# Storing x early, and adding the last scaled tiles to the output by transfers of GpSimd's queue

## The chip, the cores and the metric

The kernel runs on one core of a Trainium2 chip. Its time is the device time of one execution in microseconds (us); lower is better. The kernel before took 1996.66 us, the median of three runs (1994.56 to 1998.79). A profile shows one further execution.

## The reference, cut to what matters

Two layers work on x, 512 tokens by 1024 features in float32. Each layer has three sub-layers, a token mixer, a cross-attention into 256 memory tokens and a squared-ReLU feed-forward, and each of them ends in the same way:

```
def rms_norm(x, g):
    y = xf * lax.rsqrt(jnp.mean(xf * xf, axis=-1, keepdims=True) + NORM_EPS)
    return y * g
...
        h = rms_norm(x, ffn_pre_g[i])
        x = x + rms_norm(squared_relu_mlp(h, w_up[i], w_down[i]), ffn_post_g[i])
    return x
```

So the output is x as it stood before the last feed-forward, plus the feed-forward's result y, scaled for each token by one over its root mean square and for each feature by a gain. The change touches only this last sum.

## The kernel before, in words

Everything is kept with features on the 128 partitions: `x_sb` and `y_sb` are eight tiles (KT = 8) of 128 features by 512 tokens, each tile 256 KB. The output in memory has the same layout (128 partitions, 8 tiles, 512 tokens), so one tile is 2 KB of contiguous bytes in a partition and two neighbouring tiles are 4 KB. There are six post-norms, numbered 0 to 5, three for each layer; post-norm 5 is that of the last feed-forward.

The program is written out by hand, engine by engine, with semaphores:

- SyncE (SP) issues nearly all transfers. Its queue in order: the inputs, then the weights unit by unit (`load_unit`, L344; 512 KB a transfer into four buffers `raw`, each refilled when VectorE has read it), the memory tokens (L367), and at the very end eight stores of x (L403), each after a wait for `x_ready`, which VectorE's addition of that tile raises. Then it waits until all eight have landed (`out_done`).
- TensorE multiplies in units of 96 matmuls (L1330). Behind the last unit it sums the squares of y over features with a matrix of ones (`statistic`, L1354).
- ScalarE splits weights (L504), squares the tiles of y (L816), and makes `rstd` of the summed squares in `root`, a logarithm (L547) and an exponential (L550).
- VectorE forms the low parts of the weights (L838), adds the partial products of the feed-forward into `y_sb` (L1257), and at the end calls `post_normed(5, ...)` eight times. Each call scales one tile of `y_sb` in place (L915, raises `y_scaled`), waits for its own write, and adds it to the tile of `x_sb` (L925, raises `x_ready`). In all earlier post-norms the same function is used, and what follows reads `x_sb`.
- GpSimd adds squares (L419) and the rotated halves of queries and keys (L434). It issues no transfer anywhere in the kernel before; its last work is three additions of squares in the last feed-forward.

The order of the work around the change is: last unit of TensorE, its last partial products added to y by VectorE, squares by ScalarE, `statistic`, `root`, eight pairs of scaling and addition, and the stores that follow them tile by tile.

`wait_added(engine, post, k)` is a wait for `x_ready` to reach 8 * post + k + 1. After post-norm 4, the cross-attention's of the second layer, nothing changes `x_sb` until post-norm 5.

Of the kernel before, what the change touches and what calls it, by code (L numbers as in the profile page):

```python
# [25 lines left out]
KT = D // P  # L26
# [112 lines left out]
def build(nc, x, mem, positions, gains, consts, lam, subln_g, da_w_qkv, da_w_o, db_w_qkv, db_w_o,  # L139
# [3 lines left out]
    ALU = mybir.AluOpType  # L143
# [6 lines left out]
    with ExitStack() as ctx:  # L150
# [3 lines left out]
        def sem(name):  # L154
            return ctx.enter_context(nc.semaphore(name))


        x_sb = sb("x_sb", [P, KT, S])
        y_sb = sb("y_sb", [P, KT, S])
# [11 lines left out]
        rstd = sb("rstd", [P, S])  # L171
# [62 lines left out]
        y_scaled = sem("y_scaled")  # L234
# [21 lines left out]
        tables = sem("tables")  # L256
        lam_sums = sem("lam_sums")
        lam_exp = sem("lam_exp")
        out_done = sem("out_done")

        class Attention:

# [65 lines left out]
        def wait_added(engine, post, k):  # L328

            engine.wait_ge(x_ready, KT * post + k + 1)  # L330
# [4 lines left out]
        @block.sync  # L335
        def _(sp):
            def load_unit(u, w, row_pair, col, ii=0, pairs=range(4)):

                for j in pairs:
                    if u > 0:  # L340

                        sp.wait_ge(w_lo_ready, ii * 8 + (4 * u + j - 3))
                    src = w[bass.ds(row_pair + j, 1), bass.ds(col, 1)]
                    sp.dma_start(raw[:, j], src[0, 0]).then_inc(raw_loaded[j], 16)  # L344

            sp.dma_start(gain[:, :, :], gains).then_inc(gain_loaded, 16)
            for n, (k, end) in enumerate(X_LOADS):
                sp.dma_start(x_sb[:, k:end, :], x[:, k:end]).then_inc(x_loaded[n], 16)
                w = tiles(da_w_qkv)
                if n in FIRST_PAIRS:  # L350
                    load_unit(0, w, 0, 0, pairs=FIRST_PAIRS[n])
            sp.dma_start(cst[:, :], consts).then_inc(small_loaded, 16)
            sp.dma_start(half[:, 0, :].bitcast(i32), positions.broadcast_to([P, S])).then_inc(small_loaded, 16)
            sp.dma_start(half[:, 1, 0:4 * DA_DQ],
                         lam.broadcast_to([P, 4 * DA_DQ])).then_inc(small_loaded, 16)
            sp.dma_start(subg[:, 0:1], subln_g).then_inc(small_loaded, 16)
            for n in range(1, 6):
                load_unit(n, w, 0, n)

            def after_attention(layer, att):  # L360

                u = UNITS[f"o{layer}"]
                w = tiles(da_w_o if layer == 0 else db_w_o)
                load_unit(u, w, 0, 0)

                sp.wait_ge(att.weighed, att.n)
                sp.dma_start(mem_sb[:, :, :], mem).then_inc(mem_loaded, 16)  # L367
                load_unit(u + 1, w, 0, 1)
                w = tiles(xa_wkv[layer])
                for n, col in enumerate((2, 3, 0, 1)):  # L370
                    load_unit(UNITS[f"kv{layer}"] + n, w, 0, col)
                for name, w in (("xq", xa_wq), ("xo", xa_wo)):
                    for n in range(2):
                        load_unit(UNITS[f"{name}{layer}"] + n, tiles(w[layer]), 0, n)
                u = UNITS[f"ff{layer}"]
                up, down = tiles(w_up[layer]), tiles(w_down[layer])
                load_unit(u, up, 0, 0)
                with sp.Fori(0, CHUNKS - 1) as c:
                    load_unit(u + 1, up, 0, c * 2 + 1, c * 2)
                    for n in range(2):  # L380
                        load_unit(u + 2 + n, down, c * 4, n, c * 2)
                    load_unit(u + 4, up, 0, c * 2 + 2, c * 2)
                u += 4 * (CHUNKS - 1)
                load_unit(u + 1, up, 0, 2 * CHUNKS - 1)
                for n in range(2):
                    load_unit(u + 2 + n, down, 4 * (CHUNKS - 1), n)

            after_attention(0, att_d)
            w = tiles(db_w_qkv)
            for h in range(2):  # L390
                u = UNITS["qkv1a" if h == 0 else "qkv1b"]
                load_unit(u, w, 0, h)
                with sp.Fori(0, GROUPS - 1) as g:
                    load_unit(u + 1, w, 0, g * 2 + (2 * GROUPS + h), g)
                    load_unit(u + 2, w, 0, g * 2 + (2 + h), g)
                load_unit(u + 2 * GROUPS - 1, w, 0, 4 * GROUPS - 2 + h)
                for g in range(GROUPS):
                    load_unit(u + 2 * GROUPS + g, w, 0, 4 * GROUPS + 2 * g + h)
            after_attention(1, att_l[1])
            for k in range(KT):  # L400

                wait_added(sp, 5, k)
                sp.dma_start(out[:, k], x_sb[:, k, :]).then_inc(out_done, 16)  # L403
            sp.wait_ge(out_done, 16 * KT)


        @block.gpsimd
        def _(pool):
# [31 lines left out]
            for layer in range(2):  # L440
                for k in range(KT):
                    square_sum(f"mem{layer}", k, mem_sq)
                for k in range(POOLED[f"mix{layer}"]):
                    square_sum(f"mix{layer}", k, sq)
                for k in range(POOLED[f"xa{layer}"]):
                    square_sum(f"xa{layer}", k, sq)

                wait_added(pool, 3 * layer + 1, KT - 1)
                pool.wait_ge(rstd_ready, STATS[f"fpre{layer}"] + 1)
                nc.gpsimd.memset(y_sb[:, :, :], 0.0).then_inc(y_cleared, 1)  # L450
                if layer == 0:
                    nc.gpsimd.memset(mask[:, :, 0:S + P], 0.0).then_inc(mask_step, 1)
                    steps = 1
                    for r in range(DIL):

                        for at, width, step, base in ((0, S, DIL, r), (S, P, 1, 0)):
                            part = mask[:, r, at:at + width]
                            for sign in (1, -1):
                                pool.wait_ge(mask_step, steps)
                                nc.gpsimd.affine_select(out=part, in_=part, compare_op=ALU.is_ge, fill=MASKED,  # L460
                                                        base=RADIUS - sign * base, pattern=[[sign, width]],
                                                        channel_multiplier=-sign * step).then_inc(mask_step, 1)
                                steps += 1

                        if r == 0:
                            pool.wait_ge(phase_ready, 1)
                        for a in range(2):
                            far = mask[:, r, S + P + a * 64:S + P + (a + 1) * 64].rearrange("p (a b) -> p a b", b=DIL)
                            nc.gpsimd.tensor_copy(far, phase4[:, :].rearrange("p (o b) -> p o b", o=1)
                                                  .broadcast_to([P, 16, DIL])).then_inc(mask_step, 1)  # L470
                            steps += 1
                    assert steps == MASK_STEPS

                for k in range(POOLED[f"ff{layer}"]):
                    square_sum(f"ff{layer}", k, sq)
                if layer == 0:
                    for name in ("qkv1a", "qkv1b"):
                        u = UNITS[name]

                        def rope_sums(kind, g, ii):  # L480
                            for m in range(HALF):
                                rope_sum(banks_out(u + kind, m, ii), (u + kind) % 2,
                                         (k1 if kind % 2 else q1)[:, g, m, :], m)

                        rope_sums(0, slice(0, 1), 0)
                        with pool.Fori(0, GROUPS - 1) as g:
                            rope_sums(1, bass.ds(g, 1), g)
                            rope_sums(2, bass.ds(g + 1, 1), g)
                        rope_sums(2 * GROUPS - 1, slice(GROUPS - 1, GROUPS), 0)


        @block.scalar
# [332 lines left out]
        def _(dve):  # L825
# [82 lines left out]
            scalings_of_y = 0  # L908
# [233 lines left out]
            for layer in range(2):  # L1142
                if layer == 1:
                    for h in range(2):
# [16 lines left out]
                        if h == 0:  # L1161
                            dve.wait_ge(mask_step, MASK_STEPS)
                        for g in range(GROUPS):
# [116 lines left out]
                if layer == 0:  # L1280
                    boundary(2, 0, "ffn_post_g", "pre1", 1, "mix_pre_g", UNITS["qkv1a"])
                else:
                    for i in range(KT):
                        post_normed(5, 1, "ffn_post_g", i)

# [312 lines left out]
                statistic(f"ff{layer}")  # L1600


MASK_STEPS = 1 + DIL * 6


# [32 lines left out]
```

## Time and profile before

| | before |
|---|---|
| median of three runs | 1996.66 us |
| the profiled execution's own time | 1997.33 us |
| its span, from the first to the last instruction | 1995.5 us |
| TensorE busy | 1930.1 us, 97% of the span |
| VectorE busy | 1000.9 us, 50% |
| ScalarE busy | 738.5 us, 37% |
| GpSimd busy | 187.1 us, 9% |
| bytes moved | 167.32 MB |

The span is what the profile's clock covers; the execution's own time is 1.83 us longer, and it lies 0.67 us above the median of the runs. A point of time in the rows below is counted from the start of the span.

### The profile page before, as it was taken

Reading aid. Unit: us, or ns where it says so; the run is one execution under the profiler, and the core shown is the slowest. Engines: PE = TensorE matmul, PEld = TensorE weight load, DVE = VectorE, ACT = ScalarE, POOL = GpSimd, SP = SyncE. Lnnn points to the kernel's source line nnn. Section 1 sums busy time; section 2 is a strip of 40 time slices with the busy share of each in tenths; the row PEclk is TensorE's granted clock in tenths of the full one; section 3 lists DMA queues with packets and bytes.
Section 4 is the critical chain, followed back from the end, with each engine's and each line's share of the span. In section 5 each row is a group of like instructions: output and inputs, shape, how many; then the busy total and the mean of one; then the engine's idle time right before and its main releaser. Section 6 shows DMA issues by size and latency. Waiting matters only on the chain.

```text
span 1995.5 us, 23552 instructions
## 1 busy us (share of the span) xinstructions
PE 1930.1 (97%) x8970; PEld 1582.9 (79%) x8970; DVE 1000.9 (50%) x1369; ACT 738.5 (37%) x1148; POOL 187.1 (9%) x139
## 2 busy tenths in 40 slices
PE   8999999999999999989999999999999999999996
PEld 6785578887888888768899888898788868888885
DVE  5958937444534334476623365333474354334444
ACT  4127846334413223332124321244453343223232
POOL 0410021000300000013300033100300000000000
PEclk9999999999999999999999999999999999999998
DMA  4320034302232223323321133310352122322331
GB/s 157 95 86 10 1 106 154 110 24 76 91 95 95 95 95 96 94 74 95 95 85 43 29 94 101 95 42 5 129 173 74 43 76 93 95 95 95 95 95 53
DMA packets 85654, 167.32 MB, mean 84 GB/s; under 512 B 5568, under 2 KB 5696, under 8 KB 85312
## 3 DMA queue, kind: packets, MB, share of 16 engines
q1 hardware_dynamic: 85568, 166.15, 26.9%
q8 instruction: 57, 0.93, 0.2%
q14 instruction: 29, 0.24, 0.0%
HBM read 164.03 MB, written 2.10 MB: 83 GB/s over the span
## 4 chain that ended last, share of the span: by engine, by line
PE 86%; DVE 6%; ACT 4%; issue 2%; POOL 1%; DMA 0%; SPq 0%; ACTq 0%; DVEq 0%; POOLq 0%
PE ps L1330 74%; PE ps L1354 2%; PE ps L1499 2%; PE ps L1390 1%; DVE half L880 1%; DVE w_lo L838 1%; PE ps L1489 1%; PE ps L1492 1%; PE ps L1553 1%; PE ps L1434 1%; DVE small L1036 1%; PE ps L1545 1%; PE ps L1428 1%; ACT w_hi L504 1%; PE ps L1314 1%
## 5 line engine op out<-in xcount | busy, mean ns | idle before, releaser
L838 DVE TENSOR_TENSOR w_lo<-raw,w_hi 128x1024 fp32r<-128x1024 f32 x304 | 377.9, 1244 | 740.6 <-ACT w_hi L504 738.7
L504 ACT ACTIVATE w_hi<-raw 128x1024 fp32r<-128x1024 f32 x304 | 321.7, 1058 | 906.2 <-PE ps L1330 900.5
L1330 PE MATMUL ps<-act_hi,w_lo 128*128 128x512 f32 x1392 | 547.4, 393 | 5.7 <-DVE w_lo L838 4.0
L1330 PE MATMUL ps<-act_lo,w_hi 128*128 128x512 f32 x1408 | 548.2, 391 | 0.0
L1330 PE MATMUL ps<-act_hi,w_hi 128*128 128x512 f32 x1392 | 541.9, 389 | 0.0
L1330 PEld LDWEIGHTS ps<-act_hi,w_lo 128*128 128x128 f32 x1392 | 261.6, 188 | 64.4 <-DVE w_lo L838 5.7
L1330 PEld LDWEIGHTS ps<-act_lo,w_hi 128*128 128x128 f32 x1408 | 266.2, 189 | 57.0 <-issue 1.9
L1330 PEld LDWEIGHTS ps<-act_hi,w_hi 128*128 128x128 f32 x1392 | 261.3, 188 | 54.7
L1330 PE MATMUL ps<-ff_hi,w_lo 128*128 128x512 f32 x512 | 201.7, 394 | 0.0
L1330 PE MATMUL ps<-ff_lo,w_hi 128*128 128x512 f32 x512 | 201.7, 394 | 0.0
L1330 PE MATMUL ps<-ff_hi,w_hi 128*128 128x512 f32 x512 | 201.7, 394 | 0.0
L419 POOL TENSOR_TENSOR sq<-sq 128x512 f32<-128x512 f32 x26 | 39.0, 1500 | 956.9 <-ACT sq L816 616.1
L1330 PEld LDWEIGHTS ps<-ff_lo,w_hi 128*128 128x128 f32 x512 | 95.7, 187 | 23.7
L1330 PEld LDWEIGHTS ps<-ff_hi,w_lo 128*128 128x128 f32 x512 | 95.8, 187 | 23.7
L1330 PEld LDWEIGHTS ps<-ff_hi,w_hi 128*128 128x128 f32 x512 | 95.7, 187 | 23.6
L880 DVE TENSOR_TENSOR half<-ps,sin_sb 64x512 f32<-64x512 f32 (+1 forms) x160 | 110.1, 688 | 2.2
L1330 PE MATMUL ps<-w_hi,act_lo 128*128 128x512 f32 x256 | 102.7, 401 | 0.0
L1330 PE MATMUL ps<-w_hi,act_hi 128*128 128x512 f32 x256 | 102.0, 399 | 0.0
L1330 PE MATMUL ps<-w_lo,act_hi 128*128 128x512 f32 x256 | 102.0, 398 | 0.0
L434 POOL TENSOR_TENSOR q<-q,half 128x512 f32<-128x512 f32 (+1 forms) x32 | 58.4, 1824 | 319.6 <-DVE half L880 319.6
L1330 PEld LDWEIGHTS ps<-w_hi,act_lo 128*128 128x128 f32 x256 | 64.4, 251 | 6.1 <-issue 0.8
L1330 PEld LDWEIGHTS ps<-w_hi,act_hi 128*128 128x128 f32 x256 | 64.5, 252 | 5.3
(155 smaller groups left out, 2134.4 us busy)
## 6 DMA issues: line engine op xcount, KB each, us to landing
raw<-in_db_w_qkv SPq DMA_DIRECT2D x72, 512.0 KB, 3.8
raw<-in_w_up SPq DMA_DIRECT2D x64, 512.0 KB, 3.8
raw<-in_w_down SPq DMA_DIRECT2D x64, 512.0 KB, 3.8
raw<-in_xa_wkv SPq DMA_DIRECT2D x32, 512.0 KB, 3.9
raw<-in_da_w_qkv SPq DMA_DIRECT2D x24, 512.0 KB, 3.7
raw<-in_xa_wq SPq DMA_DIRECT2D x16, 512.0 KB, 3.9
raw<-in_xa_wo SPq DMA_DIRECT2D x16, 512.0 KB, 3.7
raw<-in_da_w_o SPq DMA_DIRECT2D x8, 512.0 KB, 3.7
```

Of the source, the lines that this page charges most:

```text
L419: nc.gpsimd.tensor_tensor(squares[:, 0, :], squares[:, 0, :], squares[:, k, :], ALU.add).then_inc(sq_summed, 1)
L434: nc.gpsimd.tensor_tensor(dst, dst, half[:, n % 2:n % 2 + 1, :], ALU.add).then_inc(rope_done, 1)
L504: nc.scalar.activation(w_hi[:, g % 2], raw[:, g % 4], ACT.Copy).then_inc(w_hi_ready, 1)
L838: nc.vector.tensor_tensor(w_lo[:, g % 2], raw[:, g % 4], w_hi[:, g % 2].bitcast(f32), ALU.subtract).then_inc(w_lo_ready, 1)
L880: last = nc.vector.tensor_tensor(half[to:to + swap, m % 2:m % 2 + 1, :], src[at:at + swap], sin_sb[at:at + swap], ALU.mult)
L1036: nc.vector.tensor_reduce(small[:, t % 2, 2:2 + count], scores, AX.X, ALU.max, negate=True).then_inc(a.taken, 1)
L1314: nc.tensor.matmul(ps[:, s + m, :], weights[:, 0, 0, c], hi[:, 0], start=(weights is w_hi), stop=False)
L1330: last = nc.tensor.matmul(ps[:, s + m, 0:width], left, right, start=(k == 0 and n == 0 and not early), stop=(k == KT - 1 and n == 2))
L1354: last = nc.tensor.matmul(ps[:, stat_bank(name), 0:width], ones[:, :], squares[:, k, :], start=(k == order[0]), stop=(k == order[-1]))
L1390: last = nc.tensor.transpose(a.turn_banks(n, b), a.e[:, n % (a.lag + 1), b * P:(b + 1) * P], ident[:, :])
L1428: last = nc.tensor.matmul(ps[:, 2 * (t % 2) + c, :], q0[r, h, s * P:(s + 1) * P], k0[r, h, :], start=True, stop=True)
L1499: last = nc.tensor.matmul(ps[:, a.out_bank(h), r * P:(r + 1) * P], v1[:, g, tile, h * P:(h + 1) * P], p_of(a, n, b), start=(b == 0), stop= ...
```

## The change

SyncE no longer stores eight tiles behind eight additions. As soon as its weight loads are issued it waits for the last tile of post-norm 4 and stores the whole of `x_sb`, 2 MB, in one transfer (`x_stored`). VectorE's last loop only scales: eight instructions on `y_sb`, without a wait between them and without the additions into `x_sb`. GpSimd, behind its last additions of squares, waits until x has landed, and then for each pair of scaled tiles issues a transfer of 512 KB that adds `y_sb` to what stands in the output. Four of these are counted in `out_added`, for which SyncE waits at the end. The number of scalings that `y_scaled` has counted before the last loop is written down as a constant, 32.

```diff
-            for k in range(KT):
-
-                wait_added(sp, 5, k)
-                sp.dma_start(out[:, k], x_sb[:, k, :]).then_inc(out_done, 16)
-            sp.wait_ge(out_done, 16 * KT)
+            wait_added(sp, 4, KT - 1)
+            sp.dma_start(out, x_sb[:, :, :]).then_inc(x_stored, 16)
+            sp.wait_ge(x_stored, 16)
+            sp.wait_ge(out_added, 16 * (KT // 2))
...
+            pool.wait_ge(x_stored, 16)
+            for k in range(0, KT, 2):
+                pool.wait_ge(y_scaled, SCALED_BEFORE_LAST + k + 2)
+                nc.gpsimd.dma_start(out[:, k:k + 2], y_sb[:, k:k + 2, :], accum_op=ALU.add).then_inc(out_added, 16)
...
                 else:
+                    assert scalings_of_y == SCALED_BEFORE_LAST
                     for i in range(KT):
-                        post_normed(5, 1, "ffn_post_g", i)
+                        nc.vector.scalar_tensor_tensor(
+                            y_sb[:, i, :], y_sb[:, i, :], gcol(1, "ffn_post_g", i), rstd[:, :],
+                            ALU.mult, ALU.mult).then_inc(y_scaled, 1)
...
+SCALED_BEFORE_LAST = 4 * KT
```

## Rows read from the trace of the kernel before

**Rows 1.** The page's first part: busy time, share of the span and instructions.

```profile
PE 1930.1 (97%) x8970; PEld 1582.9 (79%) x8970; DVE 1000.9 (50%) x1369; ACT 738.5 (37%) x1148; POOL 187.1 (9%) x139
```

**Rows 2.** The chain that ended last, from 1980 us: start us, us, what.

```profile
1980.50 0.70 ACT rstd L547
...
1981.22 0.64 ACT rstd L550
...
1981.89 0.76 DVE y_sb L915
...
1982.67 0.69 DVE x_sb L925
1983.37 0.67 DVE y_sb L915
...
1992.40 0.69 DVE x_sb L925
```

**Rows 3.** SyncE's waits from 1980 us: queue, line, releaser, total, times, longest.

```profile
SPq L403 <- DVE x_sb L925: 45.2, 8, 38.0
SPq L150 <- DMA out<-x_sb: 1.7, 1, 1.7
```

**Rows 4.** The output's transfers: duration ns, first and last start us; then time to landing.

```profile
L403 SPq DMA_DIRECT2D out<-x_sb x8: 332/332/361, 1983.4 to 1993.1; - x8
...
DMA to landing us min/median/max: 2.0/2.0/2.0
```

**Rows 5.** Short windows of the last store: us, busy engines, PEclk, DMA share, GB/s.

```profile
1993.60:1993.80 0.20, 0.00 (x0) 0.00 (x0) 0.00 (x0) 0.00 (x0) 0.00 (x0) 0.50 0.00 0
1993.80:1994.00 0.20, 0.00 (x0) 0.00 (x0) 0.00 (x0) 0.00 (x0) 0.00 (x0) 0.50 0.21 82
1994.00:1994.20 0.20, 0.00 (x0) 0.00 (x0) 0.00 (x0) 0.00 (x0) 0.00 (x0) 0.50 1.07 410
...
1994.40:1994.60 0.20, 0.00 (x0) 0.00 (x0) 0.00 (x0) 0.00 (x0) 0.00 (x0) 0.50 0.97 369
1994.60:1994.80 0.20, 0.00 (x0) 0.00 (x0) 0.00 (x0) 0.00 (x0) 0.00 (x0) 0.50 0.23 72
```

**Rows 6.** Windows of the start, where many transfers queue; columns as in rows 5.

```profile
5.00:10.00 5.00, 1.58 (x4) 1.32 (x5) 1.89 (x2) 2.56 (x4) 0.00 (x0) 1.00 1.02 390
10.00:15.00 5.00, 5.00 (x16) 3.94 (x15) 3.41 (x5) 5.00 (x9) 0.00 (x0) 1.00 1.03 383
```

**Rows 7.** SyncE's queue from 1900 us, in time: start us, us, what, count.

```profile
1906.56 38.83 SPq L344 DMA_DIRECT2D raw<-in_w_down  x8
1983.39 10.05 SPq L403 DMA_DIRECT2D out<-x_sb  x8
```

**Rows 8.** Transfers by line: count, KB each, median us from issue to landing.

```profile
raw<-in_w_down SPq DMA_DIRECT2D x64, 512.0 KB, 3.8
...
mem_sb<-in_mem SPq DMA_DIRECT2D x2, 1024.0 KB, 4.9
out<-x_sb SPq DMA_DIRECT2D x8, 256.0 KB, 2.0
x_sb<-in_x SPq DMA_DIRECT2D x3, 512.0 KB, 7.4
```

**Rows 9.** ScalarE in time from 1950 us: start us, us, line, what, idle before.

```profile
1965.07 1.06 ACT L504 ACTIVATE w_hi<-raw 128x1024 fp32r<-128x1024 f32 x1 [3.50 <-PE ps L1330]
```

**Rows 10.** GpSimd in time, from 46 us and from 1646 us; columns as in rows 9.

```profile
46.08 1.30 POOL L434 TENSOR_TENSOR q<-q,half 128x512 f32<-128x512 f32 x1 [44.42 <-DVE half L880]
49.60 2.34 POOL L434 TENSOR_TENSOR q<-q,half 128x512 f32<-128x512 f32 x1 [2.22 <-DVE half L880]
...
1966.73 3.24 POOL L419 TENSOR_TENSOR sq<-sq 128x512 f32<-128x512 f32 x2 [3.79 <-ACT sq L816]
```

**Rows 11.** VectorE in time beside those of rows 10; columns as in rows 9.

```profile
46.73 2.79 DVE L880 TENSOR_TENSOR half<-ps,sin_sb 32x512 f32<-32x512 f32 x4
49.55 1.23 DVE L838 TENSOR_TENSOR w_lo<-raw,w_hi 128x1024 fp32r<-128x1024 f32 x1
```

More of the change, by code:

```diff
@@ L258, in build @@
         lam_exp = sem("lam_exp")
-        out_done = sem("out_done")
+        x_stored = sem("x_stored")
+        out_added = sem("out_added")
         class Attention:
```

## The prediction

> **What bounds the kernel now.** I read the page's first part first: the matmul engine is busy for 97% of the span [rows 1], so nothing shortens the kernel but less matmul work or a shorter stretch without matmuls, and the change leaves all matmuls alone. The second view is the chain that ended last, at its end. The reader is to see there that behind the last statistic ScalarE's two steps of the root stand, then one scaling and one addition of VectorE in turn, with nothing between them, from 1981.89 us until the last addition ends at 1992.40 + 0.69 = 1993.09 [rows 2]. The third view is SyncE's waits: each of the eight stores waited for its addition, and at the end SyncE waited 1.7 us for the last store to land [rows 3]. So the tail is VectorE's chain, 11.20 us, then one store of 256 KB: issued at 1993.1 and landed 2.0 us later, at 1995.1 [rows 4]; 0.4 us of closing follow to the span's 1995.5. The question is only how 13.2 us, from 1981.89 to 1995.1, come out in another form.
>
> Windows of the last store split its 2.0 us [rows 5]: no byte until about 1993.95, some 0.85 us behind the issue; then about 0.7 us of movement near 400 GB/s; then 0.45 us to the landing. At the start of the kernel, where transfers queue, reads hold 383 to 390 GB/s over 10 us [rows 6]. I take 394 GB/s as the most that this core's transfers move, since shares of 0.97 to 1.07 in both views say that the transfer engines are full there.
>
> **The change, part by part.**
>
> *VectorE.* Eight additions of 0.69 us and the short gaps ahead of them go. Eight scalings stay. The first takes 0.75 to 0.76 us, and a following one adds 0.67 to the chain [rows 2], so tiles are ready at 1982.64 + 0.67 n: the first pair at 1983.31, then 1984.65, 1985.99 and the last at 1982.64 + 7 x 0.67 = 1987.33. That is 1993.09 - 1987.33 = 5.76 us earlier than the last addition before. If the overlap is lost, at 0.76 each, the last is ready at 1987.97.
>
> *The early store of x.* SyncE's last weight load is issued at 1906.56 + 38.83 = 1945.4 [rows 7]; the store of 2 MB follows at once, since post-norm 4 is long past. At 394 GB/s it moves for 5.3 us; with a load ahead of it (3.8 us to landing [rows 8]) and the fixed parts of rows 5 it lands by about 1956. GpSimd waits for it, behind its additions that end at 1966.73 + 3.24 = 1969.97 [rows 10], and it first needs x in the output at 1983.31, so there are 27 us to spare. What else could it disturb? Only the last weight tiles: the last of them is read at 1965.07 [rows 9], nearly 20 us after its load was issued. I cost the store at nothing; its cover is the last unit's matmuls, and without it the cost would be the 5.3 us and the fixed parts. The eight stores that it replaces were under VectorE's chain but the last, which is the 2.0 us above. Nothing is queued behind GpSimd's new waits but these transfers, and nobody waits for them but SyncE at the end.
>
> *The four adding transfers.* No row shows a transfer of GpSimd's queue, or one that adds. I need two prices.
>
> First, from issue to first byte. The nearest row is SyncE's store, 0.85 us [rows 5]; that is the low end of what I take. GpSimd has to prepare the transfer itself. The high end is 0.85 plus 1.4, by the longest that one of its plain additions of 128x512 takes alone (1.30 us [rows 10]). I take 0.85 + 0.9 = 1.75. Only the first counts if the transfers then queue: preparation goes on under the one before.
>
> Second, the movement t of 512 KB. Low end: a plain copy, 524288 / 394000 = 1.33 us. An adding transfer reads y from the core's memory and also the old output, two reads for one write. If the reading side of the 16 engines carries both, t is 2 x 1.33 = 2.66 us. High end: the slowest 512 KB of the trace, x's loads at 7.4 us to landing in a full queue [rows 8], less 1.3 us of fixed parts, so 6.1. I take 2.66, because the rows show transfer engines that are full at 394 GB/s of plain copies, and a second read can't be free for a full engine; it is nearer to the low end.
>
> The Trainium skill bears on this. Its page Collectives: The Full Stack (The bandwidth ceiling: the fold count and why AG ≠ RS ≠ AR) says that a reduction in the transfer engines is half as fast as a copy because it reads two sources through the same queue, and not because the addition costs. The trace has no adding transfer to agree or disagree; by that rule the sum is the one below, without it t would be open between its ends.
>
> *The sum.* First byte at 1983.31 + 1.75 = 1985.06. Transfers of 2.66 us are slower than the 1.34 us in which VectorE delivers a pair, so they queue: end at 1985.06 + 4 x 2.66 = 1995.70. Add 0.45 to land and 0.4 of closing: 1996.55, against 1995.5. VectorE's 5.76 us are given back, because 2 MB of additions now begin only when the first pair is scaled. The change in the span is +1.05 us; with the short end of the start (0.85) it is +0.15, with the long one +1.55. The profiled execution took 1997.33 us, 1.83 over its span, so it becomes 1998.4; it stood 0.67 above the median, so against the runs I say 1997.7, rounded to 1998.
>
> A measurement of this kernel can tell about 0.2%, 4 us, from no change: "same" reaches from 1992.7 to 2000.7. The change is even where t is (1995.5 - 0.85 - 1985.06) / 4 = 2.40 us, and slower by 4 us from t = 3.40.
>
> **The rivals.**
>
> *A, the transfers keep up (faster).* Reads of the two sources run side by side and t is 1.33. Then each pair's transfer is done when the next pair is ready, and only the last counts: 1987.33 + 1.75 + 1.33 + 0.45 + 0.4 = 1991.26, 4.2 us less, 1992.4 against the median; with a start as short as SyncE's, 1991.5. For it: stores one after another already reach 390 GB/s, and reading and writing are two sides of an engine. Against it: full shares in rows 5 and 6.
>
> *B, the adding is slow (slower).* Each 4 KB row is read, added and written at half the rate again, t = 5.3 us, by waiting for the old value before the write or by a slow adder. End: 1985.06 + 21.3 + 0.85 = 2007.2, 11.7 us more, 2008.4. It decides from t = 3.4 us. For it: x's 512 KB loads took 7.4 us in a full queue, and no row shows that reads and writes of the same bytes overlap. Against it: plain transfers, in rows 5 and 6, run at full share in either direction.
>
> *C, VectorE locks GpSimd out (slower).* The trace shows such a lock: an addition of GpSimd took 1.30 us beside a VectorE instruction with one input from PSUM, and 2.34 us where it began with L838, which has both inputs in SBUF; it took 1.04 us more, about what was left of L838 when it began [rows 10, 11]. The eight scalings have two such inputs and stand without a gap. If they hold up GpSimd's preparation, the first byte comes at 1987.33 + 1.75 = 1989.08 and the end at 1989.08 + 10.64 + 0.85 = 2000.6, 5.1 us more, 2001.7. Against it: GpSimd was held in a reading instruction there. The Trainium skill (SBUF — State Buffer, Who interferes with whom) says that a VectorE instruction with two inputs in SBUF holds up GpSimd's reads, not instructions that only write; rows 10 agree with its first half (2.34 us for 1.30), and no row shows the second. By it C doesn't happen.
>
> *D, the change doesn't do what it says.* The early store isn't landed at 1983.31 and everything slides. It would have to take over 37 us; 2 MB at 394 GB/s take 5.3.
>
> **How the numbers follow.** The forecast (t near 2.7) 0.45, A 0.15, B 0.28, C 0.09, D 0.03. B has much, since the price of adding is the one number that no row bounds well, and nothing hides it. Predicted time 1998. A gives 1992.4, so the range begins at 1992; B gives 2008.4 and a little above it, so it ends at 2010; A with the shortest start and B with t over 5.7 are left out. The forecast's own range, t from 2.4 to 3.4, is 1997 to 2001. Faster by over 0.2% is A, 0.15; within it is the forecast, 0.45; slower is B, C and D, 0.40.
>
> **What the changed profile would show.** VectorE's last scaling ends near 1987.3 and no addition into x_sb follows it. The store of 2 MB starts near 1945.4 and lands before 1960. GpSimd's first transfer is issued within 0.1 us of 1983.3, and under C at 1987.3 or with nothing moving before it. The share of the transfer engines is full from about 1985.1 to 1995.7; under A there are gaps between four short bursts of 1.3 us, under B a stretch of over 20 us. TensorE's stretch to 1980.5 is unchanged. I am wrong if the four transfers take less than 2.4 us each, or more than 3.4, or if they leave gaps though pairs are ready, since then it is GpSimd's preparation that sets the pace.

## The result: slower by 0.17%, with the transfers at half rate as forecast and a lag that was not

Twenty runs of each kernel: 2001.71 us median after (1997.28 to 2003.82), 1997.55 us before (1994.41 to 1999.70). The ratio is 1.0017 with a 95% interval from 1.0011 to 1.0024, so 3.4 us slower, between 2.2 and 4.8; the two medians lie 4.2 us apart. The profiled execution took 2002.83 us with a span of 2001.0.

The two profiled executions differ by 1.6 us before the tail even starts: the root ends at 1983.43 us in one and at 1981.86 in the other. Over all fourteen profiles of this study that point lies between 1978.8 and 1983.4 us, and even the two of the changed kernel differ by 1.8. So I compare tails, from the end of the root to the end of the span. The changed kernel's is 2001.0 - 1983.43 = 17.6 us, that of before 1995.5 - 1981.86 = 13.6 us: 3.9 us longer (differences of tails are taken before rounding), which the timed ratio bears out.

The changed kernel's chain of waits, its end (start us, us, what), which answers to [rows 2]:

```profile
1982.79 0.64 ACT rstd L555
...
1983.45 0.75 DVE y_sb L1290
1984.20 0.66 DVEq L150
1984.87 2.66 DVE y_sb L1290 x4
1987.53 0.28 issue
1987.81 0.84 POOL out L494
1988.65 0.46 issue
1989.12 0.88 POOLq L150
```

The reader is to see that the additions (L925 before) are gone, and that the chain passes to GpSimd and then stops at 1990.0, 11 us ahead of the end: the rest is movement of bytes, which no engine's chain shows. GpSimd's and VectorE's instructions in time, and then the output's transfers with their time to landing, against [rows 4]:

```profile
1983.45 5.39 DVE L1290 SCALAR_TENSOR_TENSOR y_sb<-y_sb,gain,rstd 128x512 f32<-128x512 f32 x8 [4.98 <-ACT rstd L555]
...
1985.50 1.90 POOL L494 DMA_DIRECT2D out<-y_sb  x2 [13.97 <-DVE y_sb L1290]
1987.81 0.84 POOL L494 DMA_DIRECT2D out<-y_sb  x1 [0.41 <-DVE y_sb L1290]
1989.14 0.86 POOL L494 DMA_DIRECT2D out<-y_sb  x1 [0.48 <-DVE y_sb L1290]
```

```profile
L494 POOL DMA_DIRECT2D out<-y_sb x4: 840/878/1000, 1985.5 to 1989.1; - x4
L402 SPq DMA_DIRECT2D out<-x_sb x1: 467/467/467, 1947.0 to 1947.0; - x1
...
DMA to landing us min/median/max: 5.8/9.1/11.4
```

Eight scalings take 5.39 us (5.44 forecast). The last adding transfer is issued at 1989.1 and lands 11.4 us later. Windows of the tail, whose last two columns are the transfer engines' share and the GB/s, against [rows 5]. A window counts a packet whole where it starts, so a share can pass 1, and does so most in the short window in which the first packets of all engines start together:

```profile
1986.80:1987.00 0.20, 0.00 (x0) 0.00 (x0) 0.20 (x2) 0.00 (x0) 0.20 (x1) 0.50 0.00 0
1987.00:1987.20 0.20, 0.00 (x0) 0.00 (x0) 0.20 (x1) 0.00 (x0) 0.20 (x1) 0.50 4.10 307
...
1987.00:1989.00 2.00, 0.00 (x0) 0.00 (x0) 1.84 (x3) 0.00 (x0) 1.24 (x2) 0.50 1.07 129
1989.00:1998.00 9.00, 0.00 (x0) 0.00 (x0) 0.00 (x0) 0.00 (x0) 0.86 (x1) 0.50 1.04 200
1998.00:2000.00 2.00, 0.00 (x0) 0.00 (x0) 0.00 (x0) 0.00 (x0) 0.00 (x0) 0.50 0.11 20
```

The last three of these lines are the result. From 1989 to 1998 us the share is full (1.04) while only 200 GB/s move, half of the 394 at which the same engines copy. Ahead of that stand 2 us at 129 GB/s, and behind it 2 us in which a share of 0.11 moves the last 40 KB. One engine of the 16 is a share of 0.06.

The trace also keeps every packet of the transfers, here one for each 4 KB row. A plain packet takes 0.162 us in the median (plain copies from the same queue, below), an adding one 0.328: the factor of two again. But 39 of the 512 adding packets take over 0.43 us, all of them in the first 6 us of movement, and the longest takes 2.41 us. The last six packets follow one after another, from 1998.36 to 2000.24 us. The trace doesn't say which engine a packet belongs to; that the last ones are the backlog of an engine which such a long packet held up is my reading of it.

### The profile page after: what moved, and what is told of

Its sections match the earlier page's. It is cut to its first block, busy times and chain, and to the rows that moved or that the text cites. A ratio compares the mean times of both kernels' runs of the same rounds, so it can differ in the third digit from the quotient of the medians.

```text
span 2001.0 us, 23543 instructions
## 1 busy us (share of the span) xinstructions
PE 1931.3 (97%) x8970; PEld 1583.9 (79%) x8970; DVE 995.4 (50%) x1361; ACT 738.5 (37%) x1148; POOL 190.7 (10%) x143
## 4 chain that ended last, share of the span: by engine, by line
PE 86%; DVE 6%; ACT 4%; issue 2%; POOL 1%; DMA 0%; POOLq 0%; DVEq 0%; SPq 0%; ACTq 0%
PE ps L1338 74%; PE ps L1362 2%; PE ps L1507 2%; PE ps L1398 1%; DVE half L885 1%; DVE w_lo L843 1%; PE ps L1497 1%; PE ps L1500 1%; PE ps L1561 1%; PE ps L1442 1%; DVE small L1041 1%; PE ps L1553 1%; PE ps L1436 1%; PE ps L1322 1%; ACT w_hi L509 1%
```

## The experiments

My theory was the forecast's: an adding transfer fills the engines and gets half a copy's rate, so 2.1 MB need over 10 us, and that stands on the path since it can't begin before the first pair is scaled. The rivals: GpSimd's queue is slow for any transfer; VectorE's scalings hold up GpSimd's preparation; the early store costs time; each transfer has a price of its own. A table of all comes first. The tail is from one profile each; the last column is what the timed ratio makes of 1997.6 us. The two kernels of plain copies leave the addition of x out. Where nothing else is said a ratio rests on eleven runs of the kernel named (twenty of the changed one), against runs of the kernel before taken beside them: on seven for plain copies from SyncE, five for adding when all is scaled, four for plain loads beside. Where tails are compared with each other, 0.6 us is what two profiles of one kernel differ by.

| kernel | ratio (95% interval) | tail us | tail less 13.6 | by ratio, us |
|---|---|---|---|---|
| changed | 1.0017 (1.0011 to 1.0024) | 17.6; again 18.2 | +3.9; +4.6 | +3.4 |
| plain copies, GpSimd's queue | 0.9981 (0.9972 to 0.9990) | 10.0 | -3.7 | -3.8 |
| plain copies, SyncE's queue | 0.9973 (0.9962 to 0.9985) | 8.4 | -5.2 | -5.4 |
| adding only when all is scaled | 1.0036 (1.0022 to 1.0050) | 21.0 | +7.3 | +7.2 |
| before, with the early store | 0.9998 (0.9989 to 1.0007) | 13.6 | 0.0 | -0.4 |
| two transfers of four tiles | 1.0017 (1.0008 to 1.0026) | 17.0 | +3.4 | +3.4 |
| eight transfers of one tile | 1.0012 (1.0003 to 1.0022) | 16.5 | +2.8 | +2.4 |
| two tiles by adding transfer | 0.9990 (0.9981 to 0.9999) | 12.2 | -1.4 | -2.0 |
| four tiles by adding transfer | 1.0005 (0.9996 to 1.0014) | 14.8 | +1.2 | +1.0 |
| plain loads beside | 1.0044 (1.0029 to 1.0059) | 21.0 | +7.4 | +8.8 |
| TensorE adds eight tiles | 1.0012 (1.0003 to 1.0021) | 15.4 | +1.8 | +2.4 |
| TensorE adds five tiles | 0.9992 (0.9983 to 1.0001) | 11.6 | -2.0 | -1.6 |

**Plain copies from GpSimd's queue.**

```diff
-                nc.gpsimd.dma_start(out[:, k:k + 2], y_sb[:, k:k + 2, :], accum_op=ALU.add).then_inc(out_added, 16)
+                nc.gpsimd.dma_start(out[:, k:k + 2], y_sb[:, k:k + 2, :]).then_inc(out_added, 16)
```

> The changed kernel with its four transfers made plain copies: y overwrites the output, the addition of x is left out. Tail is meant from the end of the root (rstd) to the end of the span: 13.6 us before, 17.6 us after. Theory (an adding transfer reads two sources, so full transfer engines give half the rate): the four copies move at 380 to 400 GB/s, 1.3 us each, keep up with VectorE's pairs, and the tail is 10 to 12 us, some 6 us under the changed kernel. Rival (the software queue is slow for any transfer): still near 205 GB/s, tail 16 to 18 us.

Its windows (columns as above):

```profile
1987.00:1990.50 3.50, 0.00 (x0) 0.00 (x0) 0.32 (x1) 0.00 (x0) 0.53 (x1) 0.50 0.96 380
1990.50:1990.80 0.30, 0.00 (x0) 0.00 (x0) 0.00 (x0) 0.00 (x0) 0.00 (x0) 0.50 0.91 369
1990.80:1991.00 0.20, 0.00 (x0) 0.00 (x0) 0.00 (x0) 0.00 (x0) 0.00 (x0) 0.50 0.08 21
```

The same bytes from the same queue in the same pieces move at 380 GB/s, and the end is sharp: no lag. The tail is 10.0 us. No packet takes over 0.24 us. So it is the adding that halves the rate and that brings the long packets and the lag, and not GpSimd's queue. The theory stands, that rival falls.

**Plain copies from SyncE's queue.**

```diff
+            for k in range(0, KT, 2):
+                sp.wait_ge(y_scaled, SCALED_BEFORE_LAST + k + 2)
+                sp.dma_start(out[:, k:k + 2], y_sb[:, k:k + 2, :]).then_inc(out_added, 16)
...
-            pool.wait_ge(x_stored, 16)
-            for k in range(0, KT, 2):
-                pool.wait_ge(y_scaled, SCALED_BEFORE_LAST + k + 2)
-                nc.gpsimd.dma_start(out[:, k:k + 2], y_sb[:, k:k + 2, :], accum_op=ALU.add).then_inc(out_added, 16)
```

> As the plain copies of y from GpSimd's queue, but issued by SyncE in the same pairs behind the same scalings; the addition of x is left out. It separates GpSimd's queue from the shape. Theory: same movement, 1.3 us each; the first byte comes 0.85 us behind the issue and nothing lags at the end, so the tail is about 5.4 + 0.85 + 1.33 + 0.45 + 0.4 = 8.4 us. If GpSimd's queue costs nothing more than SyncE's, both kernels of plain copies have the same tail.

```profile
1986.00:1990.00 4.00, 0.00 (x0) 0.00 (x0) 2.47 (x4) 0.00 (x0) 0.00 (x0) 0.50 1.00 400
```

The tail is 8.4 us, as expected. The two kernels of plain copies differ by 1.6 us: that is the price of GpSimd's queue on this path. Most of it is the time from issue to landing of a transfer, 2.7 us in the median here and 3.7 there.

**Adding only when all eight tiles are scaled.**

```diff
-                pool.wait_ge(y_scaled, SCALED_BEFORE_LAST + k + 2)
+                pool.wait_ge(y_scaled, SCALED_BEFORE_LAST + KT)
```

> The changed kernel, its four adding transfers issued only when all eight tiles are scaled. Theory (GpSimd's preparation isn't held up by VectorE's scalings): the issues are 0.85 to 0.9 us each as in the changed kernel, and the whole is later by the 4.0 us that the first issue is later, tail 21.5 us. Rival (VectorE's instructions with two inputs in SBUF hold up the preparation, so that starting early gains little): issues well under 0.85 us, the first byte under 1.6 us behind the first issue, tail 18 to 19 us.

GpSimd in time, in this kernel:

```profile
1987.07 3.65 POOL L494 DMA_DIRECT2D out<-y_sb  x4 [17.95 <-DVE y_sb L1290]
```

and windows of it:

```profile
1988.00:1990.00 2.00, 0.00 (x0) 0.00 (x0) 0.00 (x0) 0.00 (x0) 2.00 (x4) 0.50 0.80 84
1990.00:1999.50 9.50, 0.00 (x0) 0.00 (x0) 0.00 (x0) 0.00 (x0) 0.73 (x1) 0.50 1.05 197
```

With VectorE idle, GpSimd's four preparations take 3.65 us together, 0.9 each (their single records overlap), as they do beside the scalings in the changed kernel, and the first byte comes 1.6 us behind the first issue in both. VectorE doesn't hold them up; the rival called C in the prediction falls. The rate in the middle is much the same, 197 GB/s. The tail is 21.0 us, 3.4 more than the changed kernel's where 4.0 was expected; the end is less ragged here, 1.4 us of lag where the changed kernel has 2.1.

**The early store alone.**

```diff
+            wait_added(sp, 4, KT - 1)
+            sp.dma_start(out, x_sb[:, :, :]).then_inc(x_stored, 16)
+            sp.wait_ge(x_stored, 16)
             for k in range(KT):
...
+                    dve.wait_ge(x_stored, 16)
                     for i in range(KT):
                         post_normed(5, 1, "ffn_post_g", i)
```

> The kernel before with the early store of x alone, and its eight last stores as they were (they overwrite it). Theory: the 2 MB store under the last unit costs nothing, ratio 1.000 within 0.0007, tail 13.6 us. Rival (part of the 4 us is the early store, that delays the last weight tiles or slows the matmuls): 1 to 2 us slower, with a gap in the matmuls after 1946 us.

VectorE's last loop waits here until the early store has landed. Ratio 0.9998, the same tail of 13.6 us. In the changed kernel the store is issued at 1947.0 us and moves from about 1948 to 1955, beside the last weight load and under unbroken matmuls:

```profile
1948.00:1955.00 7.00, 7.00 (x32) 5.61 (x31) 2.61 (x3) 1.06 (x1) 0.00 (x0) 1.00 0.94 367
```

**Four tiles, and one tile, to a transfer.** Only the step of the loop and its counts change (`range(0, KT, 4)`; `range(0, KT, 1)`).

> The changed kernel with two adding transfers of four tiles (1 MB) instead of four of two. Tail from the end of the root to the end of the span, 17.6 us in the changed kernel. Theory (2.1 MB move at some 205 GB/s whatever the cut, and only the first issue's time counts): the first group is ready 1.35 us later, so the tail is 18.9 us. Rival (each of GpSimd's transfers costs time of its own at the start or the end): fewer of them win back 0.9 us or more, tail 18 us or less.

> The changed kernel with eight adding transfers of one tile (256 KB). Theory: the first tile is ready 0.67 us earlier and preparation (0.85 us each in the changed kernel) stays ahead of 1.3 us of movement each, so the tail is 16.9 us. Rival (a price for each transfer, or preparation that sets the pace): 18 us or more, with the transfer engines' share under 0.9 in the middle.

Four tiles: 17.0 us, not the 18.9 of the theory but where the rival was to show (18 or less); the ratio is that of the changed kernel. One tile: 16.5 us, by the theory (16.9 expected) and against the rival (18 or more). A window of four tiles, then those of one tile:

```profile
1988.60:1996.00 7.40, 0.00 (x0) 0.00 (x0) 0.00 (x0) 0.00 (x0) 0.00 (x0) 0.50 1.04 213
```

```profile
1981.00:1983.00 2.00, 0.00 (x0) 0.00 (x0) 2.00 (x4) 0.00 (x0) 2.00 (x5) 0.50 0.66 86
...
1985.00:1993.00 8.00, 0.00 (x0) 0.00 (x0) 0.00 (x0) 0.00 (x0) 2.42 (x3) 0.50 1.11 195
1993.00:1994.00 1.00, 0.00 (x0) 0.00 (x0) 0.00 (x0) 0.00 (x0) 0.00 (x0) 0.50 0.72 129
```

The middle stays near half rate whatever the cut (195, 193 to 200 and 213 GB/s for one, two and four tiles to a transfer). What the cut changes is the two ends, and not in one direction (tails of 16.5, 17.6 to 18.2, 17.0 us). Much of that is the lag. Counted from when fewer than eight packets are under way until the last has ended, it is 0.4 us with one tile, 2.1 and 2.6 in the two profiles with two, and 0.6 with four. A price for each transfer would put eight of them last; they came first. So that rival falls as the explanation of the 3.4 us. The timed intervals of the three kernels overlap, and no order of the cuts is shown.

**Two and four tiles by adding transfer, the others as before.** GpSimd's loop runs to `m`; the early store covers only `out[:, 0:m]`; VectorE scales tiles 0 to m - 1 and then runs `post_normed` for the others, which SyncE stores one by one.

```diff
-            for k in range(0, KT, 2):
+            for k in range(0, 2, 2):
                 pool.wait_ge(y_scaled, SCALED_BEFORE_LAST + k + 2)
...
+                    for i in range(2, KT):
+                        post_normed(5, 1, "ffn_post_g", i)
```

> Mixed: tiles 0 and 1 are only scaled and added by one transfer of GpSimd's queue; tiles 2 to 7 are scaled and added by VectorE and stored by SyncE as in the kernel before. Theory: the adding transfer (2.6 us) is done long before VectorE's last addition, so VectorE's chain sets the end again and is shorter by two additions: 13.6 - 2 x 0.71 = 12.2 us of tail, 1.4 us faster than before, ratio 0.9993. Rival (an adding transfer lags at the end by some us on one engine and delays the stores behind it): 13 us or more.

> Mixed: tiles 0 to 3 by two adding transfers, tiles 4 to 7 by VectorE and SyncE. VectorE's chain would end 2.8 us earlier, at a tail of 10.8 us. Theory (transfer engines at half rate for adding): from the first byte, 3.7 us behind the root, they have 5.3 us of adding and 2.7 us of stores to move, 11.7, and 0.85 to land and close: tail 12.5 us, bound by the transfer engines again, ratio 0.9994. If plain stores overtake the adding transfers, VectorE's 10.8 us show instead.

Two tiles: tail 12.2 us, ratio 0.9990, the only kernel with an addition in transfers that beats the one before, by an interval that ends just under 1 (0.9999) and a tail as expected (12.2). Of its transfers none takes longer than 6.3 us to land, so the adding one, issued at 1982.9, has landed by 1989.2, ahead of the last store's issue at 1990.7. The stores beside it are held up, 3.8 us to landing in the median for 2.0 before, but the last one isn't:

```profile
L407 SPq DMA_DIRECT2D out<-x_sb x6: 332/332/357, 1983.8 to 1990.7; - x6
...
L499 POOL DMA_DIRECT2D out<-y_sb x1: 992/992/992, 1982.9 to 1982.9; - x1
DMA to landing us min/median/max: 2.0/4.5/6.3
```

Four tiles: 14.8 us, not 12.5. Plain stores were expected to queue behind the adding transfers or to pass them. They share the engines, and then the lag is there again; the last packets to move, one at a time, are those of plain stores, which don't get past the adding ones on the engine that is behind:

```profile
1983.00:1985.00 2.00, 0.00 (x0) 0.00 (x0) 1.93 (x4) 0.00 (x0) 1.03 (x2) 0.50 0.72 76
1985.00:1989.00 4.00, 0.00 (x0) 0.00 (x0) 3.31 (x5) 0.00 (x0) 0.00 (x0) 0.50 1.05 203
1990.00:1992.00 2.00, 0.00 (x0) 0.00 (x0) 0.00 (x0) 0.00 (x0) 0.00 (x0) 0.50 1.02 371
1992.00:1994.00 2.00, 0.00 (x0) 0.00 (x0) 0.00 (x0) 0.00 (x0) 0.00 (x0) 0.50 0.18 70
```

The middle of my sum holds (half rate, then plain rate); the two ends, the slow first 2 us (76 GB/s, with some 0.6 us still empty) and the share of 0.18 for the last 2, are what I had not put in.

**Plain loads beside the adding transfers.**

```diff
+            sp.wait_ge(y_scaled, SCALED_BEFORE_LAST + 2)
+            for j in range(4):
+                sp.dma_start(raw[:, j], tiles(w_down[1])[j, 0]).then_inc(beside[j], 16)
+            for j in range(4):
+                sp.wait_ge(beside[j], 16)
```

> The changed kernel, and SyncE issues four plain loads of 512 KB (weights into the free raw buffers) as soon as the first pair is scaled; nothing reads them. Theory (the adding transfers fill the engines, by their two reads): 2.1 MB at 394 GB/s is 5.3 us more to move, and the tail goes from 17.6 to about 22.5 us. Rival (an adding transfer leaves the reading side of an engine idle while it adds, so that plain loads slip in between): tail 18 to 19.5 us, with over 300 GB/s moved in the middle.

21.0 us, between the two: 2.8 to 3.5 us longer than the changed kernel's two tails, where the theory had 5.3 us for the loads. By the timed ratios it is 5.4 us longer (1.0044 for 1.0017, four runs). Its windows:

```profile
1985.00:1990.00 5.00, 0.00 (x0) 0.00 (x0) 2.77 (x5) 0.00 (x0) 3.02 (x4) 0.50 0.95 281
1990.00:2001.00 11.00, 0.00 (x0) 0.00 (x0) 0.00 (x0) 0.00 (x0) 0.00 (x0) 0.50 1.06 233
```

The loads move first, from 1984.9 us, and the first adding packet comes only at 1989.3, 4.9 us behind its issue where the changed kernel has 1.6. After that the engines stay at a full share and move 233 GB/s of both kinds together: a plain transfer finds no room beside an adding one in which it is free. In return the ragged ends are gone. No adding packet takes over 0.72 us, and the lag is 0.3 us; so this tail is shorter than 22.5. This doesn't tell the second read from a slow adder, since either would fill the engine.

**The changed kernel once more.**

> The changed kernel once more, for a second profile of the same code. If the 2 us at the end of its transfers, in which a share of only 0.04 to 0.08 of the transfer engines moved the rest, belong to the kernel, they stand here too and the tail is 17.6 us; if they vary from run to run, the tail is 15.5 to 17 us, by the same 205 GB/s.

```profile
1985.00:1987.00 2.00, 0.00 (x0) 0.00 (x0) 2.00 (x4) 0.00 (x0) 1.41 (x2) 0.50 0.96 113
1987.00:1996.40 9.40, 0.00 (x0) 0.00 (x0) 0.02 (x1) 0.00 (x0) 0.86 (x1) 0.50 1.04 193
1996.40:1999.00 2.60, 0.00 (x0) 0.00 (x0) 0.00 (x0) 0.00 (x0) 0.00 (x0) 0.50 0.11 22
```

The slow start and the lag stand here too (tail 1999.8 - 1981.6 = 18.2 us; 51 packets over 0.43 us, the longest 3.12). They belong to the kernel.

**TensorE adds.** For all eight tiles:

```diff
+            for i in range(KT):
+                if i == KT - 1:
+                    pe.wait_ge(ln_done, STATS["ff1"] + 1)
+                nc.tensor.matmul(ps[:, SUM_BANKS[i], :], ident[:, :], x_sb[:, i, :], start=True, stop=False)
+            for i in range(KT):
+                pe.wait_ge(y_scaled, 4 * KT + i + 1)
+                nc.tensor.matmul(ps[:, SUM_BANKS[i], :], ident[:, :], y_sb[:, i, :],
+                                 start=False, stop=True).then_inc(pe_added, 1)
...
+                    for i in range(KT):
+                        act.wait_ge(pe_added, i + 1)
+                        nc.scalar.activation(x_sb[:, i, :], ps[:, SUM_BANKS[i], :], ACT.Copy).then_inc(x_out, 1)
```

> The kernel before with another way round VectorE's additions: VectorE only scales the eight tiles; TensorE, idle in the tail, adds in PSUM (identity times x ahead of time, then identity times the scaled y), ScalarE copies each sum out and SyncE stores it plainly tile by tile. No early store, no transfer that adds. Theory (what bounded the kernel before was VectorE's chain, and what bounds the changed one is the adding transfers): the last tile is scaled 5.4 us behind the root, plus a matmul of 0.4 to 0.9 us, a copy of 0.65 us, a store of 2.0 us and 0.4 us of closing: tail 9 to 9.5 us, 4 us less than before, ratio 0.998. Rival (TensorE at its lower clock or ScalarE becomes the chain): 10 to 12 us.

A miss: tail 15.4 us. TensorE in time:

```profile
1977.91 7.03 PE L1614 MATMUL ps<-x_sb,ident 128*128 128x512 f32 x16
...
1984.78 7.03 PE L1617 MATMUL ps<-y_sb,ident 128*128 128x512 f32 x16
```

A plain float32 matmul of 128x512 shows as two records and takes 7.03 / 8 = 0.88 us even at the full granted clock (1.00 in these 14 us), so sixteen of them, 14 us, are longer than VectorE's eight additions. I had taken one record, 0.43 us, for the whole, in spite of my upper end of 0.9. TensorE never stood idle here; in the kernel before it did, and the granted clock was 0.50 at the end of the tail [rows 5].

With five tiles on TensorE and three on VectorE (`BY_PE = 5`; SyncE stores in the order 0, 5, 1, 2, 6, 3, 7, 4):

> Where all eight additions ran on TensorE the chain was TensorE's: 16 matmuls in float32 of 0.86 us each. Here TensorE adds five tiles (five matmuls of x from the end of the statistic, then five of the scaled y), VectorE scales these first and then scales and adds the other three, SyncE stores each plainly in the order in which they come. Counted from the end of the root: VectorE's last addition at 0.75 + 4 x 0.67 + 3 x 1.39 = 7.6 us; TensorE's last sum at 10 x 0.86 less the 1.4 us by which it starts earlier, 7.2, and its copy at 7.8. Plus 2.0 us of store and 0.4 of closing: tail 10.2 us against 13.6 before and 17.6 in the changed kernel, so 3.4 us faster than before, ratio 0.9983. If the two chains get in each other's way (stores that queue, TensorE at its lower clock): 11 to 13 us.

The tail is 11.6 us and the ratio 0.9992, whose interval just includes 1: not shown to be faster. The last copy ended 7.8 us behind the root, as worked out. What made it longer than the 10.2 expected was the next thing in line, the stores (their issues and landings, and a window of them):

```profile
L407 SPq DMA_DIRECT2D out<-x_sb x8: 332/461/648, 1983.4 to 1987.2; - x8
...
DMA to landing us min/median/max: 2.1/2.7/3.0
```

```profile
1985.00:1989.00 4.00, 1.15 (x3) 0.19 (x1) 1.52 (x3) 1.26 (x3) 0.00 (x0) 1.00 1.03 383
```

They were ready so close together that they queued: 2.1 MB at 383 GB/s are 5.5 us from the first byte on, and a store landed 2.7 us behind its issue in the median for 2.0 before. From here a shorter tail needs output that leaves earlier, and not only additions that are faster.

## Why the prediction was right, and where it was short

- **What bounds the kernel.** VectorE's chain bounded the tail: plain copies from SyncE with the additions left out save 5.2 us, and the forecast had VectorE 5.76 us earlier.
- **VectorE's part.** The pair was ready 1.44 us behind the root (1.45 forecast), the last tile 5.4.
- **The early store at nothing.** Shown: 0.9998.
- **Half rate.** The step on which everything hung. The forecast took 197 GB/s (2.66 us for 512 KB); 193 to 203 were measured in the full stretches of five profiles (changed kernel twice, all scaled, one tile, four tiles added), against 380 to 400 of plain copies; two transfers of four tiles had 213. By the packet it is 0.328 us for 0.162. The Trainium skill's rule of two source reads (Collectives: The Full Stack, The bandwidth ceiling: the fold count and why AG ≠ RS ≠ AR), which the page states for reductions between cores and not for this path, gives this factor of two. That the cause is the second read and not the adder wasn't shown; the two weren't told apart.
- **Start of the transfers, mis-sized.** From the pair being ready to the first byte: 1.75 us forecast, 2.2 measured (1984.87 to 1987.07). Of it 0.6 us stood ahead of the issue, which the forecast had within 0.1 us of the pair. Then 2 us at 129 GB/s in place of 197 cost another 0.7.
- **End of the transfers, the term that was missing.** I closed the sum with 0.45 + 0.4 us, the plain store's, and let all engines end together. The closing held: 0.8 us from the end of the last packet. Ahead of it stood 2.2 us of lag, for which the sum had no term. The sum by measured terms: 3.6 to the first byte, 11.0 to 1998.0, 2.2 of lag, 0.8 at the end, 17.6 us of tail against the 14.7 forecast.
- **The rivals.** A (no second read) fell with the half rate. B (slower than half) fell in the stretch itself; only the first 2 us and the lag are slower than half. C fell with the scalings moved away, and in the changed kernel the first byte came at 1987.1 us, 1.8 ahead of the end of the last scaling. The 2001.7 that C had priced is the measured median by chance. D fell with the early store, whose bytes had moved by 1955.
- **Two readings of rows that don't hold.** Rival A leans on stores that reach 390 GB/s one after another; that row [rows 6] is of the loads at the start. And the long end of the start takes 1.4 us from a row of 1.30 [rows 10], which moves that end by 0.1 us and the forecast not at all.

The direction and the mechanism were right and the size was not: 1.05 us forecast, 3.4 by the timed ratio. By the ratio that is within the 4 us that I called no change; by the medians, 4.2 apart, it is just outside, and 2001.7 lies just above the forecast's own 1997 to 2001. That it still fell between 1992 and 2010 it owes to the width that B had asked for. And what filled that range was not a larger t in the full stretch, for which I had opened it, but the two ends.

## What to carry to other kernels

An addition that a transfer makes isn't free work beside the engines: here it cost the transfer engines twice a plain copy, so 2 MB of it moved for 13 us with the lag, where the additions that it replaced had held VectorE's chain for 5.8. It pays only for the part that finishes while something else still sets the end (here two of eight tiles, ratio 0.9990); for the last bytes it lost in every form tried here. When the ends of a chain are swapped, price the new last step by its time to landing, its laggard engine included, and ask what the output's own bytes need: 2.1 MB took 5.3 to 5.5 us at 383 to 394 GB/s, however fast they were computed.

## What the runs showed of the hardware that I had not expected

- Adding transfers start slowly and end raggedly: in the changed kernel's two profiles 129 and 113 GB/s for the first 2 us at a share of 1.07 and 0.96, and then 2.1 and 2.6 us of lag at the end. Plain copies from the same queue show neither.
- Both come with single long packets among the early ones. Over the median they cost 17.7 us together in the changed kernel, 1.1 for each of 16 engines, and where one stands out it is about as long as the lag, which fits one engine held up but doesn't show it: longest 2.41, 3.12, 2.19 and 1.51 us with a lag of 2.1, 2.6, 2.2 and 1.4 (changed kernel twice, four tiles added, all scaled). With one tile to a transfer the longest was 1.93 us and the lag only 0.4, so it matters too how they fall on the engines. Beside plain loads there were none over 0.72 us. Why a packet takes so long stays open.
- By the packet adding costs about the same factor at two sizes: 0.328 us for 0.162 with 4 KB, 0.178 for 0.086 with 2 KB (plain ones in the kernel before).
- GpSimd's preparation of a transfer of 512 KB that adds takes 0.84 to 1.0 us, of a plain one 0.53 (0.71 the first), and the adding one is not held up by VectorE's instructions with two inputs in SBUF, although an addition of GpSimd's was [rows 10, 11]. The first issue stood 0.6 us behind the tile that it waited for.
